# Mixer heads: VectorE weighs each tile of scores within the turn that made its argument

## The chip, the cores and the metric

The kernel runs on one core of a Trainium2 chip. TensorE (PE in the profile; its weight loads are PEld) multiplies matrices, VectorE (DVE), ScalarE (ACT) and GpSimd (POOL) work on tiles, and SyncE (SP) issues the DMAs. The engines run side by side, each through its own list of instructions in order, and wait for each other at semaphores. The metric is the device time of one execution in microseconds (us); lower is better.

## What is computed

The reference runs two blocks of a model over 512 tokens of width 1024. The change lies in the first block's token mixer, in the four heads of its gated linear attention. In the reference's chunked form this is, for each head and each chunk:

```python
d = jnp.where(causal, b[..., :, None] - b[..., None, :] + logi[..., None, :], -jnp.inf)
m_t = jnp.maximum(inter, jnp.max(d, -1))
p = jnp.exp(d - m_t[..., None]) * jnp.einsum('bhctd,bhcsd->bhcts', q, k)
num = (s_int[..., None] * jnp.einsum('bhcvk,bhctk->bhctv', c_prev, q)
       + jnp.einsum('bhcts,bhcsv->bhctv', p, v))
den = s_int * jnp.einsum('bhck,bhctk->bhct', n_prev, q) + jnp.sum(p, -1)
h = num / jnp.maximum(jnp.abs(den), jnp.exp(-m_t))[..., None]
```

The heads are then standardized over their 128 features (mean and variance), scaled, and multiplied by a sigmoid gate. The kernel has no chunks here: it takes all 512 tokens of a head at once, so that `p` is one causal matrix, and `num` and `den` are its products with the values and with ones.

## The kernel before

**Tiles and turns.** Everything is feature-major, 128 partitions by up to 512 columns. The causal matrix of a head is worked in four tiles of 128 keys by 512, 384, 256 and 128 queries. One tile is a turn; `n` counts the 16 turns, `h, j = divmod(n, 4)` is the head and the tile in it. All engines run through the same loop over `n` in `mlstm`, each with its own part:

- VectorE makes the tile's argument (`argument`, L1535 and L1536) in `e[:, n % 4]` (tile `m_e`), which frees ScalarE to take its exponential (L1684).
- TensorE makes the scores in one of two PSUM banks (L1579).
- VectorE weighs: `weigh(n)` multiplies scores and exponential (L1522, scores from PSUM) and then the first 128 columns with the causal mask (L1524, two inputs in SBUF), and reports `prob_ready`.
- TensorE multiplies the tile with the values (L1417) and with ones (L1418), in `nums(n)`, one turn later. In turn n it runs: the scores of n, four steps of a fill, `nums(n - 1)`, a sum for the norm of the head before, a product for the pair, four more steps of a fill.

**What else stands in a turn.** The *fill* is a projection of the block's input (3 products a step, L435 to L437) with streamed weights, one job of eight steps a turn; VectorE takes most of them out of PSUM (`shifted`, L1809 and L1811), ScalarE every fourth. The *norm* of head h - 1 runs through the turns of head h in steps 0 to 3 (`norm_values`: L1498 in step 1, L1503 and L1505 in step 2, the reciprocal L1509 in step 3), and `norm_end` (L1512, L1514) ends it in the turn after. The *pair* is the preparation of the next stage's operands (`Operands.dve`), one pair per four turns: in turns with j = 1 its step 0 (L1888 to L1898, which waits for gates from ScalarE, after TensorE's L1836 and L1852), with j = 2 step 1 (L1902, behind a root of ScalarE's, and the reciprocal L1903), with j = 3 step 2 (L1905, L1906, L1908), and with j = 0 of the next head step 3 (L1913, L1914, L1915, L1920). L1908 is what TensorE's L1845 waits for, which stands in a turn with j = 0 between the scores and the fill.

**Streamed weights.** In each turn ScalarE, after its exponential, casts the high part of the next weights' tile (L387), and GpSimd makes its low part behind that (L396, both inputs in SBUF, 128x1024). SyncE loads the tile after next as a slot of the ring becomes free.

**What sets the order.** The order is written by hand: on each engine the instructions run as the loops give them out, and every dependency is a semaphore. In VectorE's loop before, turn n begins with `weigh(n - 1)`, then come `argument(n)`, `norm_end`, the take of the fill's job, `norm_values` and the pair's step. In the last turn, n = 15, `weigh(15)` stands behind the take as well.

Of the kernel before, what the change touches and what calls it, by code (L numbers as in the profile page):

```python
# [30 lines left out]
ST = S // P  # L31
# [6 lines left out]
MW, MH, MHD = 512, 4, 128  # L38
# [1308 lines left out]
def mlstm(k, h_in, arriving, early, qk, v, o, rkv, wa, gd, lora, lora_g, pairs, rooms, core, raw, norm):  # L1347
# [57 lines left out]
    def prep(n):  # L1405

        return [(pairs[(n - 1) // ST], (n - 1) % ST)] if 0 < n <= MH * ST else []
# [86 lines left out]
    def norm_values(dve, chain, h, step):  # L1494
        if step == 1:

            dve.wait_ge(*meaned.ge(2 * h + 1))
            nc.vector.scalar_tensor_tensor(out=hm[:], in0=k.banks[SPREAD], scalar=-1.0 / MHD, in1=hm[:],  # L1498
                                           op0=ALU.mult, op1=ALU.add).then_inc(*G("centred_ready").inc())
        if step == 2:  # L1500

            dve.wait_ge(*G("den_ready").ge(h + 1))
            chain(nc.vector.tensor_tensor(rs, rs, lowb[:], ALU.max))  # L1503
            dve.wait_ge(*meaned.ge(2 * h + 2))
            nc.vector.scalar_tensor_tensor(out=rs, in0=k.banks[SPREAD], scalar=1.0 / MHD, in1=rs,  # L1505
                                           op0=ALU.mult, op1=ALU.add).then_inc(*G("var_ready").inc())
        if step == 3:
            dve.wait_ge(*rooted.ge(h + 1))
            chain(nc.vector.reciprocal(rs, rs))  # L1509

    def norm_end(dve, chain, h):
        chain(nc.vector.scalar_tensor_tensor(out=hm[:], in0=hm[:], scalar=k.vec("m_norm_g", h), in1=rs, op0=ALU.mult, op1=ALU.mult))  # L1512
        dve.wait_ge(*fill.taken(names.index(f"o{h}")))
        nc.vector.tensor_tensor(y[:, h, :], hm[:], o[:, h, :], ALU.mult).then_inc(*normed.inc())  # L1514

    def weigh(dve, chain, n):
        h, j = divmod(n, ST)
        ed = e[:, n % 4, 0:width[j]]

        dve.wait_ge(*expd.ge(n + 1))  # L1520
        dve.wait_ge(*sent.ge(n + 1))
        chain(nc.vector.scalar_tensor_tensor(out=ed, in0=k.banks[SCORE[n % 2]][:, 0:width[j]], scalar=MHD ** -0.5, in1=ed,  # L1522
                                             op0=ALU.mult, op1=ALU.mult))
        nc.vector.tensor_tensor(e[:, n % 4, 0:P], e[:, n % 4, 0:P], k.const("key_le_query"), ALU.mult).then_inc(*prob.inc())  # L1524

    def argument(dve, chain, n):
        h, j = divmod(n, ST)
        if j == 0:

            dve.wait_ge(*G("spread_taken").ge(top_nth(h)))  # L1530
        if n >= 4:

            dve.wait_ge(*summed.ge(n - 3))
        ed = e[:, n % 4, 0:width[j]]
        chain(nc.vector.tensor_scalar(ed, topb[:, j * P:S], u_col[:, j, h:h + 1], -1.0, ALU.subtract, ALU.mult))  # L1535
        nc.vector.tensor_scalar(ed, ed, 0.0, None, ALU.min).then_inc(*made.inc())  # L1536

    with k.stage() as block:
        @block.sync
        def _(sp):  # L1540
            k.load_inputs(sp)
            k.prefetch(sp, fill.first[GATES_JOB])
            k.load_tables(sp)
            k.load_small(sp, lora[:], k.lora[:, 0, :])
            k.load_small(sp, lora_g[:], k.lora[:, 1:3, :])
            k.lora_landed = k.small_load()
            k.prefetch(sp, k.used)

            sp.wait_ge(*G("operands_made").ge(PAIRS))
            sp.wait_ge(*G("values_made").ge(2 * PAIRS))  # L1550
            k.load_small(sp, raw, k.memT)
            k.raw_landed = k.small_load()
# [166 lines left out]
        @block.vector  # L1719
        def _(dve):  # L1720
            chain = Chain(dve, G("dve_step"))
            nc.vector.memset(hm[:, 0:1], 0.0).then_inc(*G("gains_ready").inc())
            early.dve(dve, 0, 4)
            k.split_first(dve)
            early.dve(dve, 4, DT)
            arriving.dve_adds(dve, 0, 4)
            arriving.dve_adds(dve, 4)
            arriving.dve_roots(dve)

            dve.wait_ge(*arriving.named("turned_ready").ge(1))  # L1730
            nc.vector.tensor_copy(hm[:], k.banks[arriving.turn_bank]).then_inc(*G("high_made").inc())
            arriving.dve_parts(dve, 0, DT)
            c = VECTORS["mu_rkv"]
            chain(nc.vector.tensor_scalar(k.keep_share[:], k.vecs[:, c:c + 15], -1.0, 1.0, ALU.mult, ALU.add))
            for t in range(2 * MH):
                fill.take(dve, chain, t)
            fill.take(dve, chain, GATES_JOB)
            dve.wait_ge(*G("gate_taken").ge(1))
            nc.vector.scalar_tensor_tensor(out=tmp, in0=fpre, scalar=-1.0, in1=fpre, op0=ALU.mult,
                                           op1=ALU.max).then_inc(*G("abs_ready").inc())  # L1740
            fill.take(dve, chain, WA)

            dve.wait_ge(*G("ln_ready").ge(1))
            chain(nc.vector.scalar_tensor_tensor(out=fpre, in0=fpre, scalar=0.0, in1=tmp, op0=ALU.min, op1=ALU.subtract))
            chain(nc.vector.tensor_tensor_scan(run, fpre, fpre, 0.0, ALU.add, ALU.bypass))
            nc.vector.tensor_tensor(u, ipre, run, ALU.subtract).then_inc(*G("rows_ready").inc())
            dve.wait_ge(*G("rows_ready").ge(1))
            chain(nc.vector.tensor_tensor_scan(top, u, u, 0.0, ALU.max, ALU.max))
            nc.vector.tensor_tensor(low, top, run, ALU.add).then_inc(*G("rows_ready").inc())

            dve.wait_ge(*G("floor_ready").ge(1))
            chain(nc.vector.tensor_scalar(low, low, EPS, 1e-37, ALU.mult, ALU.max))
            nc.vector.tensor_scalar(low, low, 1e37, None, ALU.min).then_inc(*G("floor_ready").inc())

            dve.wait_ge(*G("turned_ready").ge(1))
            nc.vector.tensor_copy(u_col[:].rearrange("p t h -> p (t h)"), k.banks[SPREAD][:, 0:ST * MH]).then_inc(*G("turned_taken").inc())
            dve.wait_ge(*G("turned_taken").ge(1))
            dve.wait_ge(*k.tables_landed)
            for n in range(MH * ST):
                h, j = divmod(n, ST)  # L1760
                if n:
                    weigh(dve, chain, n - 1)
                argument(dve, chain, n)
                if h >= 2 and j == 0:
                    norm_end(dve, chain, h - 2)
                if n and jobs[UNITS + n - 1].engine == "dve":
                    fill.take(dve, chain, UNITS + n - 1)
                if n == MH * ST - 1:
                    weigh(dve, chain, n)
                if h:  # L1770
                    norm_values(dve, chain, h - 1, j)
                if n == MH * ST - 1:
                    norm_end(dve, chain, h - 1)
                for pair, step in prep(n):
                    pair.dve(dve, step, arrived)
            fill.take(dve, chain, LAST)
            norm_values(dve, chain, MH - 1, 1)
            last_pair.dve(dve, 3, arrived)
            core.dve_masks(dve, 0, 0, 0)
            norm_values(dve, chain, MH - 1, 2)  # L1780
            core.dve_masks(dve, 0, 0, 1)
            core.dve_masks(dve, 0, 0, 2)
            norm_values(dve, chain, MH - 1, 3)
            norm_end(dve, chain, MH - 1)
            for step in range(3):
                core.dve_masks(dve, 0, 1, step)
            core.dve_rest(dve, 0)
            core.dve_group(dve, 1)
# [2622 lines left out]
```

## Time and profile before

| | |
|---|---|
| median of 3 runs | 1659.35 us (1658.65 to 1659.6) |
| the profiled execution's own time | 1663.44 us |
| its span in the trace | 1661.6 us |
| TensorE busy | 1597.8 us, 96% |
| VectorE busy | 911.7 us, 55% |
| ScalarE busy | 690.3 us, 42% |
| GpSimd busy | 712.0 us, 43% |
| mean granted clock of TensorE | 0.994 |

The heads run from about 97 to 256 us of the span. A busy share over the whole span says little of them: what matters there is which wait ends last in each turn. The trace's timeline gives each instruction its start, its length, its line, and in brackets how long its engine sat idle before it and which instruction let it go. Matmul ends are modelled and overlap; the distance between two starts on TensorE is the surer measure. A row of waits adds up such idle times for one pair of lines. The profiled execution took 4.1 us more than the median; a difference worked out from its rows is set against its own time and then carried to the median.

### The profile page before, as it was taken

To read this page: it belongs to the slowest core of one execution; us is meant where nothing else is said; L and a number is where in the kernel's file an instruction comes from. 1 tells how busy PE (TensorE), PEld (TensorE's weight loads), DVE (VectorE), ACT (ScalarE), POOL (GpSimd) and SP (SyncE) were. 2 spreads that over 40 slices of the span, in tenths; PEclk is the share of its full clock that TensorE was granted. 3 is DMA by queue.
4 is the path that set the end of the run, shared out by engine and by line. 5 is a ranking of instruction groups with operands and counts; after the bars stand their busy time and mean duration, and the time that the engine had idled before them with its cause. 6 is when DMAs were issued, how large, how long until landed. Compare 5 with 4: busy or idle time off the path is not lost. (4 is left out here: it accounts for less than half of the span.)

```text
span 1661.6 us, 25020 instructions
## 1 busy us (share of the span) xinstructions
PE 1597.8 (96%) x10298; PEld 1229.7 (74%) x10298; DVE 911.7 (55%) x1464; ACT 690.3 (42%) x1184; POOL 712.0 (43%) x357
## 2 busy tenths in 40 slices
PE   6999998879999899999999999999999999999999
PEld 5876666778887688888888888476676567787787
DVE  5957878446852427556531157697536663324251
ACT  5544454324432532222233234434645465455441
POOL 4533336234652145555564446343134422463342
PEclk9999999999999999999999999999999999999999
DMA  5321111003432032333333343022112210442132
GB/s 183 137 87 51 51 51 54 4 29 91 153 113 76 26 102 76 95 96 101 102 92 105 95 133 118 23 64 64 41 57 75 89 64 26 139 156 86 51 100 79
DMA packets 39713, 138.54 MB, mean 83 GB/s; under 512 B 4400, under 2 KB 5680, under 8 KB 38320
## 3 DMA queue, kind: packets, MB, share of 16 engines
q1 hardware_dynamic: 39600, 136.94, 26.1%
q8 instruction: 82, 1.34, 0.3%
q14 instruction: 31, 0.25, 0.1%
HBM read 132.73 MB, written 4.19 MB: 82 GB/s over the span
## 5 line engine op out<-in xcount | busy, mean ns | idle before, releaser
L396 POOL TENSOR_TENSOR parts<-ring,parts 128x1024 fp32r<-128x1024 f32 (+3 forms) x250 | 581.8, 2333 | 806.6 <-ACT parts L387 806.5
L435 PE MATMUL banks<-h_hi,parts 128*128 128x512 f32 x1120 | 461.9, 412 | 3.4 <-PEq L295 3.4
L437 PE MATMUL banks<-h_hi,parts 128*128 128x512 f32 x1120 | 438.1, 391 | 0.0
L436 PE MATMUL banks<-h_lo,parts 128*128 128x512 f32 x1120 | 437.6, 391 | 0.0
L387 ACT CAST parts<-ring 128x1024 fp32r<-128x1024 f32 (+3 forms) x251 | 244.8, 979 | 134.9 <-PE banks L437 134.8
L435 PEld LDWEIGHTS banks<-h_hi,parts 128*128 128x128 f32 x1120 | 211.4, 189 | 62.4 <-issue 18.7
L436 PEld LDWEIGHTS banks<-h_lo,parts 128*128 128x128 f32 x1120 | 211.5, 189 | 46.1 <-issue 5.1
L437 PEld LDWEIGHTS banks<-h_hi,parts 128*128 128x128 f32 x1120 | 210.9, 188 | 45.2
L3130 ACT CAST ffn_act_hi<-ffn_gate 128x512 fp32r<-128x512 f32 x22 | 13.7, 622 | 162.7 <-DVE ffn_gate L3029 162.7
L435 PE MATMUL banks<-ffn_act_hi,parts 128*128 128x512 f32 x176 | 68.5, 389 | 0.0
L436 PE MATMUL banks<-ffn_act_lo,parts 128*128 128x512 f32 x176 | 68.5, 389 | 0.0
L437 PE MATMUL banks<-ffn_act_hi,parts 128*128 128x512 f32 x176 | 68.5, 389 | 0.0
L3086 DVE TENSOR_TENSOR ffn_raw<-banks,ffn_root 128x512 f32<-128x512 f32 x22 | 15.2, 691 | 86.9 <-PE banks L437 86.8
L3096 DVE TENSOR_TENSOR x<-x,banks 128x512 f32<-128x512 f32 x8 | 5.5, 687 | 88.5 <-PE banks L437 88.5
L1074 DVE SCALAR_TENSOR_TENSOR ffn_gate<-ffn_raw,vecs,ffn_gate 128x511 f32<-128x511 f32 (+1 forms) x44 | 52.5, 1192 | 1.6
L2753 ACT ACTIVATE scores<-scores,row_stats 128x128 f32<-128x128 f32 (+3 forms) x64 | 35.5, 555 | 29.9 <-DVE row_stats L2731 29.8
L1070 DVE TENSOR_SCALAR ffn_gate<-ffn_raw,vecs 128x512 f32<-128x512 f32 x22 | 40.4, 1836 | 0.8
L435 PEld LDWEIGHTS banks<-ffn_act_hi,parts 128*128 128x128 f32 x176 | 33.0, 188 | 6.9
L436 PEld LDWEIGHTS banks<-ffn_act_lo,parts 128*128 128x128 f32 x176 | 33.0, 188 | 6.9
L437 PEld LDWEIGHTS banks<-ffn_act_hi,parts 128*128 128x128 f32 x176 | 33.0, 188 | 6.7
L2741 DVE TENSOR_SCALAR scores<-scores,row_stats 128x128 f32<-128x128 f32 (+3 forms) x64 | 34.6, 540 | 2.3
L2793 ACT ACTIVATE h_hi<-x,vecs 128x512 fp32r<-128x512 f32 x16 | 11.6, 726 | 51.3 <-DVE x L3075 27.1
(607 smaller groups left out, 2979.4 us busy)
## 6 DMA issues: line engine op xcount, KB each, us to landing
ring<-weights SPq DMA_DIRECT2D x211, 512.0 KB, 3.5
ring<-weights SPq DMA_DIRECT2D x24, 256.0 KB, 2.6
x<-xT SPq DMA_DIRECT2D x4, 1024.0 KB, 5.4
ring<-weights SPq DMA_DIRECT2D x8, 384.0 KB, 3.1
x_spill<-x SPq DMA_DIRECT2D x2, 1024.0 KB, 4.8
x<-x_spill SPq DMA_DIRECT2D x1, 2048.0 KB, 9.2
outT<-x SPq DMA_DIRECT2D x8, 256.0 KB, 2.0
ring<-weights SPq DMA_DIRECT2D x8, 192.0 KB, 2.4
```

The costliest lines, as they stand in the source:

```text
L387: self.nc.scalar.copy(self.parts[:, t % PARTS, 0, 0:w], self.ring[:, t % SLOTS, 0:w]).then_inc(self.high_ready, 1)
L396: self.nc.gpsimd.tensor_tensor(self.parts[:, t % PARTS, 1, 0:w], self.ring[:, t % SLOTS, 0:w], self.parts[:, t % PARTS, 0, 0:w].bitcast(F3 ...
L435: nc.tensor.matmul(out, w.hi, x.hi, start=first, stop=False)
L436: nc.tensor.matmul(out, w.hi, x.lo, start=False, stop=False)
L437: return nc.tensor.matmul(out, w.lo, x.hi, start=False, stop=last)
L1070: chain(nc.vector.tensor_scalar(dst, bank, k.vec(f"{weights}{taps - 1}", tile), k.vec(bias, tile), ALU.mult, ALU.add))
L1074: ins = nc.vector.scalar_tensor_tensor(out=dst[:, lag:S], in0=bank[:, 0:S - lag], scalar=k.vec(f"{weights}{j}", tile), in1=dst[:, lag:S], ...
L2741: nc.vector.tensor_scalar(scores(j - 1, e), scores(j - 1, e), st[:, 3:4], None, ALU.mult).then_inc(*scaled.inc())
L2753: nc.scalar.activation(scores(j, e), scores(j, e), ACT.Exp, bias=small[:, u % NS, 1:2], scale=-1.0, accum_out=small[:, u % NS, 2:3]).then_ ...
L2793: nc.scalar.mul(self.h.hi[:, m, :], k.x[:, m, :], k.vec(self.gain, m)).then_inc(*G("h_high").inc())
L3086: nc.vector.tensor_tensor(r, bank(gate_job(f)), root, ALU.mult).then_inc(*G("gate_taken").inc())
L3130: nc.scalar.copy(act_t.hi[:, f, :], gate[:, f % GATES, :]).then_inc(*G("act_high").inc())
```

## The change

VectorE's loop loses `weigh(n - 1)` at the turn's start. `weigh(n)` now stands, in every turn, behind the take of the fill's job and ahead of `norm_values` and of the pair's step; for the last turn this is where it was. The weighing of turn n thus waits for the exponential and the scores of the same turn. No instruction is added or removed, and the other engines' lists are the same.

```diff
             for n in range(MH * ST):
                 h, j = divmod(n, ST)
-                if n:
-                    weigh(dve, chain, n - 1)
                 argument(dve, chain, n)
                 if h >= 2 and j == 0:
                     norm_end(dve, chain, h - 2)
                 if n and jobs[UNITS + n - 1].engine == "dve":
                     fill.take(dve, chain, UNITS + n - 1)
-                if n == MH * ST - 1:
-                    weigh(dve, chain, n)
+                weigh(dve, chain, n)
                 if h:
                     norm_values(dve, chain, h - 1, j)
                 if n == MH * ST - 1:
```

Lines behind the edit stand three lower in the changed kernel (L1809 becomes L1806, L1902 becomes L1899, L1908 becomes L1905). VectorE's instructions in turn 6 (head 1, j = 2), before; the first two rows weigh turn 5:

```order
L1522 SCALAR_TENSOR_TENSOR m_e<-banks,m_e 128x384
L1524 TENSOR_TENSOR m_e<-m_e,consts 128x128
L1535 TENSOR_SCALAR m_e<-top_b,u_col 128x256
L1536 TENSOR_SCALAR m_e<-m_e 128x256
L1809 TENSOR_SCALAR rkv<-banks,keep_share 128x512
L1811 SCALAR_TENSOR_TENSOR rkv<-banks,vecs,rkv 128x511
L1503 TENSOR_TENSOR y<-y,floor_b 128x512
L1505 SCALAR_TENSOR_TENSOR y<-banks,y 128x512
L1902 TENSOR_SCALAR x<-x 128x512
L1903 RECIPROCAL x<-x 128x512
```

And now, from the argument of turn 6 on; the weighing is that of turn 6:

```order
L1535 TENSOR_SCALAR m_e<-top_b,u_col 128x256
L1536 TENSOR_SCALAR m_e<-m_e 128x256
L1806 TENSOR_SCALAR rkv<-banks,keep_share 128x512
L1808 SCALAR_TENSOR_TENSOR rkv<-banks,vecs,rkv 128x511
L1522 SCALAR_TENSOR_TENSOR m_e<-banks,m_e 128x256
L1524 TENSOR_TENSOR m_e<-m_e,consts 128x128
L1503 TENSOR_TENSOR y<-y,floor_b 128x512
L1505 SCALAR_TENSOR_TENSOR y<-banks,y 128x512
L1899 TENSOR_SCALAR x<-x 128x512
L1900 RECIPROCAL x<-x 128x512
```

The weighing of 384 columns left the turn's start, and that of 256 columns stands between the fill's take (L1808) and the norm's L1503. VectorE in turn 7 (j = 3), before:

```order
L1522 SCALAR_TENSOR_TENSOR m_e<-banks,m_e 128x256
L1524 TENSOR_TENSOR m_e<-m_e,consts 128x128
L1535 TENSOR_SCALAR m_e<-top_b,u_col 128x128
L1536 TENSOR_SCALAR m_e<-m_e 128x128
L1809 TENSOR_SCALAR rkv<-banks,keep_share 128x512
L1811 SCALAR_TENSOR_TENSOR rkv<-banks,vecs,rkv 128x511
L1509 RECIPROCAL y<-y 128x512
L1905 TENSOR_TENSOR x<-x 128x512
L1906 TENSOR_TENSOR qk_60<-qk_60,x 128x512
L1908 SCALAR_TENSOR_TENSOR x<-rkv,vecs,x 128x512
```

And now:

```order
L1535 TENSOR_SCALAR m_e<-top_b,u_col 128x128
L1536 TENSOR_SCALAR m_e<-m_e 128x128
L1806 TENSOR_SCALAR rkv<-banks,keep_share 128x512
L1808 SCALAR_TENSOR_TENSOR rkv<-banks,vecs,rkv 128x511
L1522 SCALAR_TENSOR_TENSOR m_e<-banks,m_e 128x128
L1524 TENSOR_TENSOR m_e<-m_e,consts 128x128
L1509 RECIPROCAL y<-y 128x512
L1902 TENSOR_TENSOR x<-x 128x512
L1903 TENSOR_TENSOR qk_60<-qk_60,x 128x512
L1905 SCALAR_TENSOR_TENSOR x<-rkv,vecs,x 128x512
```

The weighing of turn 7 (128 columns) now stands directly ahead of the norm's reciprocal L1509, and that of turn 6 has left the turn.

## Rows read from the trace of the kernel before

**Rows 1.** Waits, 97 to 256 us: who waited for whom, us in total, times, longest.
```profile
DVE m_hm L1498 <- PE banks L1473: 13.4, 3, 6.0
...
PEld banks L1417 <- DVE m_e L1524: 6.7, 8, 1.2
...
PE banks L1417 <- DVE m_e L1524: 3.3, 8, 0.8
```

**Rows 2.** TensorE's timeline: start us, us, engine, line, operation, tiles, shape, [idle before <-releaser].
```profile
132.75 1.97 PE L1845 MATMUL banks<-x,consts 128*128 128x512 f32 x2
...
156.24 0.91 PE L1417 MATMUL banks<-m_e,m_v 128*128 128x384 f32 x2 [0.36 <-DVE m_e L1524]
...
165.60 0.70 PE L1417 MATMUL banks<-m_e,m_v 128*128 128x256 f32 x2 [0.34 <-DVE m_e L1524]
...
173.00 1.12 PE L1845 MATMUL banks<-x,consts 128*128 128x512 f32 x2 [0.37 <-DVE x L1908]
...
211.60 2.07 PE L1845 MATMUL banks<-x,consts 128*128 128x512 f32 x2 [0.36 <-DVE x L1908]
...
565.56 0.47 PE L435 MATMUL banks<-x_out_parts_hi,parts 128*128 128x512 f32 x1 [2.81 <-DVE x_out_parts_lo L1145]
```

**Rows 3.** VectorE's timeline, turns 2 and 3, 6 and 7, and 15.
```profile
120.70 0.84 DVE L1902 TENSOR_SCALAR x<-x 128x512 f32<-128x512 f32 x1 [1.89 <-ACT x L1869]
...
128.25 2.80 DVE L1906 TENSOR_TENSOR x<-x 128x512 f32<-128x512 f32 x1
...
155.31 0.56 DVE L1522 SCALAR_TENSOR_TENSOR m_e<-banks,m_e 128x384 f32<-128x384 f32 x1
...
155.90 0.29 DVE L1524 TENSOR_TENSOR m_e<-m_e,consts 128x128 f32<-128x128 f32 x1
...
156.11 0.35 DVE L1535 TENSOR_SCALAR m_e<-top_b,u_col 128x256 f32<-128x256 f32 x1
...
157.48 0.75 DVE L1811 SCALAR_TENSOR_TENSOR rkv<-banks,vecs,rkv 128x511 f32<-128x511 f32 x1
...
158.14 0.68 DVE L1503 TENSOR_TENSOR y<-y,floor_b 128x512 f32<-128x512 f32 x1
...
160.74 0.64 DVE L1902 TENSOR_SCALAR x<-x 128x512 f32<-128x512 f32 x1 [1.18 <-ACT x L1869]
...
164.79 0.42 DVE L1522 SCALAR_TENSOR_TENSOR m_e<-banks,m_e 128x256 f32<-128x256 f32 x1
...
165.46 0.28 DVE L1535 TENSOR_SCALAR m_e<-top_b,u_col 128x128 f32<-128x128 f32 x1
...
167.37 3.34 DVE L1509 RECIPROCAL y<-y 128x512 f32<-128x512 f32 x1
...
172.19 0.75 DVE L1908 SCALAR_TENSOR_TENSOR x<-rkv,vecs,x 128x512 f32<-128x512 f32 x1
...
172.86 0.28 DVE L1522 SCALAR_TENSOR_TENSOR m_e<-banks,m_e 128x128 f32<-128x128 f32 x1
...
246.48 2.26 DVE L1524 TENSOR_TENSOR m_e<-m_e,consts 128x128 f32<-128x128 f32 x1
```

**Rows 4.** ScalarE's timeline, turn 6.
```profile
157.14 1.03 ACT L387 CAST parts<-ring 128x1024 fp32r<-128x1024 f32 x1
```

**Rows 5.** GpSimd's timeline, turns 6 and 7.
```profile
158.24 2.85 POOL L396 TENSOR_TENSOR parts<-ring,parts 128x1024 fp32r<-128x1024 f32 x1 [12.81 <-ACT parts L387]
...
167.36 2.42 POOL L396 TENSOR_TENSOR parts<-ring,parts 128x1024 fp32r<-128x1024 f32 x1 [6.27 <-ACT parts L387]
```

**Rows 6.** GpSimd's timeline, turn 15.
```profile
246.16 2.44 POOL L396 TENSOR_TENSOR parts<-ring,parts 128x1024 fp32r<-128x1024 f32 x1 [6.27 <-ACT parts L387]
```

**Rows 7.** Busy time by stretch: stretch, length, each engine (instructions), PEclk, DMA share, GB/s.
```profile
130.00:140.00 10.00, 10.00 (x31) 5.81 (x30) 9.79 (x14) 3.73 (x6) 5.52 (x4) 0.83 0.28 84
210.00:220.00 10.00, 9.64 (x33) 6.49 (x33) 9.76 (x15) 3.24 (x5) 4.76 (x3) 0.83 0.29 93
565.00:575.00 10.00, 9.44 (x34) 7.64 (x35) 5.90 (x10) 5.62 (x11) 2.56 (x1) 0.83 0.16 54
```

## The prediction

> **What bounds the kernel now.** I read the waits of the mixer's heads first [rows 1], then TensorE's timeline there [rows 2], then VectorE's, ScalarE's and GpSimd's [rows 3 to 6], and the granted clock last [rows 7]. In the waits, TensorE's product of the weighed scores (L1417) waited 8 times of 16 for the mask product L1524, which ends the weighing: 6.7 us in its weight loads and 3.3 us in its matmuls [rows 1]. That is what the change can give back. VectorE had 13.4 us of waiting of its own at L1498, in three pieces, so it is not full over the whole region [rows 1].
>
> TensorE's timeline shows where each wait lies. Call a head's four turns j = 0 to 3. In head 1 the waits are at 156.24 us (turn 6, j=2, 0.36 us) and at 165.60 us (turn 7, j=3, 0.34 us), and then a third, 0.37 us at 173.00 (turn 8), which is for another VectorE row: L1908, the last of the pair's step [rows 2]. So in turns 6 and 7 TensorE and VectorE are nearly level. VectorE's rows there follow each other almost without a pause: from 155.31, where L1522 begins, to 172.94, where L1908 ends (172.19 + 0.75), it idles only 1.18 us, at L1902, for a root that ScalarE makes from what VectorE gave it [rows 3]. L1845 on TensorE starts 0.06 us behind L1908's end. **The chain that sets a head's length in its second half is VectorE's, up to L1908.** Its first half, from L1845 to the next gates, is TensorE's fills. L1845 to L1845 took 38.60 us (173.00 to 211.60) and 40.25 us (132.75 to 173.00) [rows 2].
>
> **The change part by part.** Nothing is added or removed: 16 weighings, two VectorE instructions each, move from the start of turn n+1 to turn n, behind the argument and the taking out of a fill. Seen from a turn's start, the argument comes earlier and the weighing later.
>
> *The eight waits at L1417.* The weighing that they wait for is now done a turn earlier; even with all that follows, it is over some 5 us ahead. They go. At 0.36 and 0.34 us of idle matmul time, and up to 6.7/8 = 0.84 us of weight-load time each [rows 1, 2], I take 0.55 us: 1.1 us a head. In heads 1 to 3 this is only worth something if L1908 is not late, since L1845 waits for it already.
>
> *Turn 6 on VectorE (and turns 10, 14).* Before, L1535 began at 156.11, 0.80 us behind the turn's start at 155.31; now it begins at the start, so everything that hangs on it comes 0.80 us earlier: the exponential, the cast L387 of the next weights (157.14, now 156.34), and behind it GpSimd's L396 (158.24, now 157.44) [rows 3 to 5]. The fill's L1811 ended at 158.23, now at 157.43. L1522 can start 0.09 us ahead of that end, as L1503 does now (158.14), so at 157.34; at 0.42 us for 256 columns it ends at 157.76, and L1524 starts at 157.80. L396 has been running for 0.36 us by then. What that does the trace shows: the L1524 at 246.48 took 2.26 us instead of 0.29, and ended 0.14 us behind the L396 that had begun at 246.16 (end 248.60) [rows 3, 6]. So did L1906 at 128.25, 2.80 us against the 0.68 of L1503, which has the same shape [rows 3]. Hence L1524 ends at 157.44 + 2.42 + 0.14 = 160.00, with 2.42 us the undisturbed L396 of 167.36 [rows 5]. L1503 then starts at 159.91, where it was at 158.14 (it got in 0.1 us ahead of L396): **1.77 us later**, and the root, L1902 and the reciprocal with it.
>
> That rule is also in the Trainium skill (SBUF — State Buffer, section Who interferes with whom): a VectorE instruction with two SBUF inputs and a GpSimd one that reads SBUF exclude each other for a whole instruction, and whichever starts first decides. It speaks against this change; the trace agrees by the 2.26 us above. If the two did not exclude each other, the stalls would be zero and the sum -1.6 us (worked out under the rivals).
>
> *Turn 7 (and 11).* Here the argument was 0.67 us behind the turn's start (165.46 against 164.79). L396 goes from 167.36 to 166.69. The reciprocal L1509 stood at 167.37, right behind the fill's take; without the 0.67 us it could start at 166.70. There L1522 now stands, 0.28 us for 128 columns (172.86) [rows 3], and L1524 at 167.02, 0.33 us behind L396's start. It ends at 166.69 + 2.42 + 0.14 = 169.25, and L1509 starts at 169.17: **1.80 us later**. L1522 has one SBUF input (the other is in PSUM), L1509 one; neither is held up.
>
> *Turns 8, 12 (j=0) and 5, 9, 13 (j=1).* The weighing is now ahead of L1913 to L1920 and may be stalled by the rest of an L396 too, but VectorE has its waits at L1498 right behind it, 13.4 us in three [rows 1]. Cost zero; if that cover were gone, up to 2.4 us a head. In j=1 no fill is taken by VectorE, and L1524 comes before L396: zero.
>
> *Head 0 (turns 1 to 4).* In turn 2 VectorE waited 1.89 us for the root at L1902 [rows 3], which covers the stall of 1.77 us. In turn 3, L1906 at 128.25 already lost its 2.1 us to the same L396; now L1524 loses them in its place. Nothing is lost, and the two waits at L1417 are given back: -1.1 us.
>
> *Head 3.* Turn 14 pays 1.77 us. Turn 15 already weighed twice, the second time stalled (the 2.26 us); it loses one weighing, 0.7 us. The waits of two products go, 1.1 us. I take 0 for the sum.
>
> Queues: SP issues weights behind the low parts that L396 makes, which move by under 1 us per turn; no DMA is in these waits, so zero.
>
> Sum: -1.1 + 2 x (1.77 + 1.80) + 0 = -1.1 + 7.1 = **+6.0 us** on the profiled execution's 1663.4 us. Applied to the median of 1659.35 us this is 1665.4 us. What follows the heads is bound by TensorE and VectorE in sequence, so I carry the shift through. Bounds of the one unknown size, the stall: from nothing (L1524 ahead of L396) to 2.42 us; per head 0 to 4.8 us.
>
> **The clock.** In two stretches, 130 to 140 and 210 to 220 us, the mean granted clock was 0.83 [rows 7]: a spell at the lower of the two levels (1.2 GHz). The head with the first took 1.65 us more (40.25 against 38.60 us). After the change TensorE pauses at L1845 in heads 1 and 2 for 0.37 + 0.70 + 3.57 = 4.6 us at a time. A pause of 2.81 us at 565.56 was followed by a stretch of 0.83 [rows 2, 7]. Two new spells, at 1.65 us, would add 3.3 us; two spells are there already, and the first may go, as the work shifts. I leave the number at two in the forecast and keep 3.3 us for the range.
>
> The Trainium skill (TensorE: Matmul & The Clock Gate, section Part 1: The HAM clock gate) says that an idle TensorE falls to half its clock and wins it back by work. By that the long pauses would each bring a spell, and the sum would be 9.3 us in place of 6.0.
>
> **The rivals.**
>
> *VectorE comes first.* If L396 starts over 0.36 us later than I shift it (turn 6; 0.33 us in turn 7), L1524 is through before it. For it: L1503 won just such a race by 0.1 us, at 158.14. Against it: cast and L396 both hang on the argument, as L1524 does, so the 0.36 us is a difference of fixed durations. Then a head's chain is shorter by 0.09 + 0.13 us; TensorE's waits still move to L1845, since VectorE's chain sets the pace: -1.1 - 0.5 = -1.6 us, 1657.8 us. Chance 0.08. If it wins in one of the two turns only: 6.0 - 3.6 = +2.4 us, 1661.8 us, chance 0.12.
>
> *All waits are kept as gain.* If the chain to L1908 has a slack that I don't see, the eight waits give between 3.3 and 6.7 us; 5 us, 1654.4 us. Against it: L1845 waits for L1908 already. It decides if L1908 ends no later than now by more than 0.37 us. Chance 0.06.
>
> *The stalls come, and the pauses slow the clock.* +6.0 + 3.3 = 1668.7 us. Chance 0.24, as part of slower.
>
> *The order does nothing,* because ScalarE's exponential comes too late for VectorE: no, the cast behind the exponential of turn 6 starts at 156.34, 1.1 us before the fill is taken out (157.43).
>
> **How the numbers follow.** Forecast (stalls, two spells) 0.50 at 1665.4; its own range 1664 to 1667. Stalls with slower clock 0.24. One of the stalls 0.12, none 0.08, all waits kept 0.06. A measurement of this kernel can tell some 0.2% (3.3 us) from no change, so faster 0.06, same 0.20, slower 0.74. The range runs from 1659.0 to 1669.5: it leaves out the cases at 1657.8 and 1654.4 and a little at the top.
>
> **What would show it.** In the changed kernel's trace L1524 in turns 2, 3, 6, 7, 10, 11, 14 lasts about 2.2 us and ends 0.14 us behind an L396. L1417 waits for nothing; TensorE's idle time ahead of L1845 is over 3 us in heads 1 and 2. L1845 to L1845 takes some 42.2 us from head 1 to 2, where it took 38.60. I am wrong if L1524 lasts 0.29 us in those turns, if L1845's waits stay under 1 us, or if something behind the heads gives the 6 us back.

## The result

The changed kernel is slower, by more than forecast.

| | before | changed |
|---|---|---|
| median | 1659.35 us (5 runs, 1658.65 to 1662.48) | 1672.32 us (5 runs, 1669.93 to 1673.57) |
| ratio | | 1.0065, 95% interval 1.0047 to 1.0083 |
| profiled execution: time, span | 1663.44, 1661.6 us | 1669.98, 1668.2 us |
| mean granted clock, profiled | 0.994 | 0.990 |

A second comparison on one chip with other kernels gave 1670.65 us against 1660.68 us, ratio 1.0054 (1.0039 to 1.0069). By the two ratios the loss is 10.8 and 9.0 us, by the plain medians 13.0 and 10.0 us, where I had said 6.0; the time lies above the range. The two profiled executions are only 6.5 us apart: that of the kernel before was slower than all five of its timed runs, that of the changed kernel is its second fastest. So the traces below show where the time goes, but not all of the loss.

**VectorE, turns 6 and 7 of the changed kernel** (start us, length us, engine, line), which answer to [rows 3]; lines behind the edit stand three lower (L1902 is now L1899, L1908 is L1905). Turn 6 begins with L1535, at 153.69:

```profile
153.69 0.35 DVE L1535 TENSOR_SCALAR m_e<-top_b,u_col 128x256 f32<-128x256 f32 x1
...
155.07 0.75 DVE L1808 SCALAR_TENSOR_TENSOR rkv<-banks,vecs,rkv 128x511 f32<-128x511 f32 x1
...
155.74 0.41 DVE L1522 SCALAR_TENSOR_TENSOR m_e<-banks,m_e 128x256 f32<-128x256 f32 x1
...
156.18 2.21 DVE L1524 TENSOR_TENSOR m_e<-m_e,consts 128x128 f32<-128x128 f32 x1
...
158.32 0.68 DVE L1503 TENSOR_TENSOR y<-y,floor_b 128x512 f32<-128x512 f32 x1
...
160.91 0.43 DVE L1899 TENSOR_SCALAR x<-x 128x512 f32<-128x512 f32 x1 [1.18 <-ACT x L1866]
...
164.76 0.28 DVE L1535 TENSOR_SCALAR m_e<-top_b,u_col 128x128 f32<-128x128 f32 x1
...
166.67 0.28 DVE L1522 SCALAR_TENSOR_TENSOR m_e<-banks,m_e 128x128 f32<-128x128 f32 x1
...
166.98 2.23 DVE L1524 TENSOR_TENSOR m_e<-m_e,consts 128x128 f32<-128x128 f32 x1
...
169.14 3.34 DVE L1509 RECIPROCAL y<-y 128x512 f32<-128x512 f32 x1
...
173.96 0.75 DVE L1905 SCALAR_TENSOR_TENSOR x<-rkv,vecs,x 128x512 f32<-128x512 f32 x1
```

**GpSimd there**, which answers to [rows 5]:

```profile
155.84 2.41 POOL L396 TENSOR_TENSOR parts<-ring,parts 128x1024 fp32r<-128x1024 f32 x1 [9.92 <-ACT parts L387]
...
166.67 2.40 POOL L396 TENSOR_TENSOR parts<-ring,parts 128x1024 fp32r<-128x1024 f32 x1 [8.42 <-ACT parts L387]
```

L1524 takes 2.21 and 2.23 us where it took 0.29 us, and both times L396 began ahead of it, by 0.34 and 0.31 us. Nothing else in these turns has grown: L1522 waits for nobody, and the wait for the root at L1899 is 1.18 us, as it was. Over the 16 turns L1524 takes 2.17 to 2.25 us in turns 2, 3, 4, 6, 7, 10, 11, 14 and 15, 1.72 us in turn 1, 0.72 to 0.77 us in turns 0, 8 and 12, and 0.29 us in turns 5, 9 and 13.

**TensorE.** The waits of the changed kernel, 97 to 266 us (us in total, times, longest), against [rows 1]:

```profile
PEld banks L1842 <- DVE x L1905: 12.4, 3, 5.8
...
DVE m_hm L1498 <- PE banks L1473: 10.8, 3, 4.4
...
PE banks L1842 <- DVE x L1905: 10.0, 2, 5.0
...
DVE m_e L1522 <- ACT m_e L1684: 1.8, 3, 0.6
```

L1417 is gone from the list. VectorE's wait for the exponential in the argument's own turn (L1522 for L1684) is 1.8 us in all, in three places, in turns 5, 9 and 13. L1417's place in the list is taken by L1842 (L1845 before). Its four places in TensorE's timeline, against [rows 2]:

```profile
132.79 1.13 PE L1842 MATMUL banks<-x,consts 128*128 128x512 f32 x2
...
174.77 2.07 PE L1842 MATMUL banks<-x,consts 128*128 128x512 f32 x2 [5.01 <-DVE x L1905]
...
218.29 2.08 PE L1842 MATMUL banks<-x,consts 128*128 128x512 f32 x2 [4.98 <-DVE x L1905]
...
264.53 1.02 PE L1842 MATMUL banks<-x,consts 128*128 128x512 f32 x2
```

From L1842 to L1842 it now is 41.98 us (132.79 to 174.77) and 43.52 us (174.77 to 218.29), where it was 40.25 and 38.60 us. Around the second and third product the mean granted clock stood at 1.00 and 0.83 before (170 to 180, 210 to 220 us). In the changed kernel it is (stretch, length, busy time of each engine, PEclk, DMA share, GB/s):

```profile
130.00:140.00 10.00, 10.00 (x37) 6.22 (x36) 9.83 (x13) 3.83 (x6) 4.49 (x4) 1.00 0.30 79
170.00:180.00 10.00, 5.23 (x14) 3.55 (x15) 9.76 (x13) 1.95 (x3) 2.75 (x2) 0.66 0.16 52
215.00:225.00 10.00, 6.71 (x21) 4.80 (x22) 9.76 (x14) 1.94 (x3) 3.70 (x2) 0.66 0.12 33
```

The level is the lower one (1.2 GHz) from 171.2 to 178.1 us and from 215.6 to 222.4 us: each spell begins in the pause ahead of L1842, and ends 3.3 and 4.1 us behind the product's start. Before, the two spells lasted 3.4 us each (from 132.9 and from 211.4 us).

### The profile page after: what moved, and what is told of

Its sections match the earlier page's. It is cut to its first block and busy times, and to the rows that moved or that the text cites. A ratio compares the mean times of both kernels' runs of the same rounds, so it can differ in the third digit from the quotient of the medians.

```text
span 1668.2 us, 25026 instructions
## 1 busy us (share of the span) xinstructions
PE 1599.5 (96%) x10298; PEld 1233.2 (74%) x10298; DVE 919.7 (55%) x1464; ACT 690.9 (41%) x1184; POOL 706.7 (42%) x357
## 5 line engine op out<-in xcount | busy, mean ns | idle before, releaser
L396 POOL TENSOR_TENSOR parts<-ring,parts 128x1024 fp32r<-128x1024 f32 (+3 forms) x250 | 575.8, 2309 | 819.5 <-ACT parts L387 819.3
L1074 DVE SCALAR_TENSOR_TENSOR ffn_gate<-ffn_raw,vecs,ffn_gate 128x511 f32<-128x511 f32 (+1 forms) x44 | 48.3, 1097 | 1.6
L1070 DVE TENSOR_SCALAR ffn_gate<-ffn_raw,vecs 128x512 f32<-128x512 f32 x22 | 44.2, 2011 | 0.8
```

The source lines that it names most:

```text
L396: self.nc.gpsimd.tensor_tensor(self.parts[:, t % PARTS, 1, 0:w], self.ring[:, t % SLOTS, 0:w], self.parts[:, t % PARTS, 0, 0:w].bitcast(F3 ...
L1070: chain(nc.vector.tensor_scalar(dst, bank, k.vec(f"{weights}{taps - 1}", tile), k.vec(bias, tile), ALU.mult, ALU.add))
L1074: ins = nc.vector.scalar_tensor_tensor(out=dst[:, lag:S], in0=bank[:, 0:S - lag], scalar=k.vec(f"{weights}{j}", tile), in1=dst[:, lag:S], ...
```

## Experiments

My theory: (1) L1524 is held behind L396 in the turns with j = 2 and 3, (2) that makes L1905 late and TensorE stands at L1842, and (3) its pauses lower the granted clock, which comes on top. The rivals: that weighing in the argument's own turn costs time by itself (VectorE waits for the exponential, or the pair's work comes late), and that the part of the loss that I had not forecast lies behind the heads. "Before" in each comparison is the kernel before on the same chip.

### e1: the two rows out of L396's way

```diff
-        chain(nc.vector.scalar_tensor_tensor(out=ed, in0=k.banks[SCORE[n % 2]][:, 0:width[j]], ...))
-        nc.vector.tensor_tensor(e[:, n % 4, 0:P], e[:, n % 4, 0:P], k.const("key_le_query"), ALU.mult)
+        score = k.banks[SCORE[n % 2]]
+        chain(nc.vector.tensor_tensor(score[:, 0:P], score[:, 0:P], k.const("key_le_query"), ALU.mult))
+        nc.vector.scalar_tensor_tensor(out=ed, in0=score[:, 0:width[j]], scalar=MHD ** -0.5, in1=ed, ...)
...
                 argument(dve, chain, n)
+                if h and j == 2:
+                    norm_floor(dve, chain, h - 1)
```

`norm_floor` is L1503, taken out of `norm_values` for all heads but the last.

> The changed kernel with VectorE's two rows that met GpSimd's L396 taken out of its way: the causal mask is multiplied into the scores in PSUM ahead of the weighing (so that neither row of the weighing has two SBUF inputs), and the norm's L1503 stands right behind the argument, ahead of L396. If the stalls behind L396 are the cause, the 1.8 us in the turns with j = 2 and in those with j = 3 go, 7 us in heads 1 and 2, and the pauses of 5.0 us ahead of L1842 shrink to about 1.5 us, with the low clock behind them: 1657 to 1660 us, the weighing's second row without any length over 0.8 us. If instead the wait for ScalarE's exponential in the same turn, or something behind the heads, costs the time, it stays at 1670 to 1673 us.

Measured: 1659.79 us against 1660.80 us, ratio 0.9991 (0.9981 to 1.0002). VectorE in turn 7 of e1, where the weighing is now L1527 (mask into the scores in PSUM) and L1528, with the reciprocal L1513 behind it, and GpSimd's L396 beside them:

```profile
164.66 0.29 DVE L1527 TENSOR_TENSOR banks<-banks,consts 128x128 f32<-128x128 f32 x1
...
164.99 0.29 DVE L1528 SCALAR_TENSOR_TENSOR m_e<-banks,m_e 128x128 f32<-128x128 f32 x1
...
165.20 3.34 DVE L1513 RECIPROCAL y<-y 128x512 f32<-128x512 f32 x1
...
164.66 2.42 POOL L396 TENSOR_TENSOR parts<-ring,parts 128x1024 fp32r<-128x1024 f32 x1 [6.50 <-ACT parts L387]
```

The weighing stands at the same place as in the changed kernel, L396 runs beside it, and neither row is held: 0.29 us each. TensorE's pauses ahead of the pair's product (L1849 here) are 1.17 and 1.16 us. The order that the change makes costs nothing by itself; the rows with two SBUF inputs that met L396 did. This takes the first rival away.

What I had not expected is that the low clock did not go with the long pauses. In this execution a spell of 3.4 us begins at 171.8 us, behind the pause of 1.17 us, and one of 6.8 us at 209.3 us, at the pause of 1.16 us; 5.6 us of it lie behind the product:

```profile
170.83 1.18 PE L1849 MATMUL banks<-x,consts 128*128 128x512 f32 x2 [1.17 <-DVE x L1912]
...
210.00:220.00 10.00, 9.46 (x30) 7.04 (x31) 9.37 (x15) 3.04 (x5) 5.33 (x3) 0.69 0.17 52
```

### e2: TensorE kept busy in the pauses

The changed kernel with idle products inside the pauses; they compute nothing that is used.

```diff
                 for pair, step in prep(n):
                     if step == 3:
+                        if n in (8, 12):
+                            pe.wait_ge(*G("rooted").ge(pair.p + 1))
+                            for _ in range(18):
+                                nc.tensor.matmul(k.banks[7], h_in.hi[:, 0, 0:P], h_in.hi[:, 0, :], start=True, stop=True)
                         pair.pe(pe, 2)
```

> The changed kernel with 18 idle products (128x512, into the bank that L1842 overwrites) on TensorE ahead of L1842 in turns 8 and 12, some 4.1 us each, inside the pauses of 5.0 us. The stalls on VectorE stay. If the low granted clock behind the two pauses is what made the loss larger than the 6 us of the stalls, the spells of 6.8 us at half clock are gone and the time is 1664 to 1668 us. If the rest of the loss lies behind the heads or in the stalls themselves, it stays at 1670 to 1673 us.

Measured: 1667.19 us against 1660.80 us, ratio 1.0038 (1.0025 to 1.0051). TensorE's timeline at the first pause (L1588 is the idle product, L1846 the pair's), and the granted clock in the same stretches as above:

```profile
169.35 4.38 PE L1588 MATMUL banks<-h_hi 128*128 128x512 f32 x18
...
174.41 1.13 PE L1846 MATMUL banks<-x,consts 128*128 128x512 f32 x2 [0.68 <-DVE x L1909]
...
216.37 1.13 PE L1846 MATMUL banks<-x,consts 128*128 128x512 f32 x2 [0.67 <-DVE x L1909]
```

```profile
130.00:140.00 10.00, 10.00 (x38) 6.41 (x37) 9.79 (x14) 3.83 (x6) 4.49 (x4) 1.00 0.31 97
170.00:180.00 10.00, 9.32 (x42) 7.08 (x41) 9.76 (x13) 2.70 (x5) 3.10 (x2) 1.00 0.15 51
215.00:225.00 10.00, 9.33 (x41) 6.94 (x40) 9.79 (x15) 2.66 (x4) 5.43 (x3) 1.00 0.17 54
```

The stalls on VectorE are all there, but no spell of low clock is left in the heads. From L1846 to L1846 it is 41.96 us (174.41 to 216.37) where the changed kernel had 43.52: 1.56 us of clock. From the third to the fourth it is 44.32 us (216.37 to 260.69) against 46.24 us (218.29 to 264.53): 1.92 us. So 3.5 us of the changed kernel's time in these two pieces are the clock's, and with idle work in their place the loss is 6.4 us; its interval, 4.2 to 8.5 us, holds the 6.0 that the stalls were forecast to cost. The intervals of the ratios of e2 and of the changed kernel overlap slightly. The trace separates them, and so does the clock of the timed runs: 0.994 to 0.997 in the six of e2, 0.989 to 0.993 in the eleven of the changed kernel.

### e3: the weighings of j = 0 and 1 moved alone

The edit is shown against the changed kernel.

```diff
+            moved = lambda n: n % ST < 2 or n == MH * ST - 1
...
+                if n and not moved(n - 1):
+                    weigh(dve, chain, n - 1)
                 argument(dve, chain, n)
...
-                weigh(dve, chain, n)
+                if moved(n):
+                    weigh(dve, chain, n)
```

> One part of the change alone: the weighing moves into its own turn only for j = 0 and 1 (and turn 15, where it was); for j = 2 and 3 it stays at the next turn's begin. By the theory of the stalls none is left, since the moved weighings of j = 1 come before L396 and those of j = 0 lie in VectorE's slack, and L1908's chain loses the weighing of 0.8 us at the begin of the turn with j = 2: -2 to -3 us against the kernel before, 1656 to 1658 us. If moving any weighing ahead of the pair's work costs time (the operands late), it is slower than before, 1662 us or more.

Measured: 1656.36 us against 1660.80 us, ratio 0.9974 (0.9964 to 0.9985): clearly faster than before. In its trace L1524 takes 0.29 us in turns 5 to 7, and TensorE waits 0.35 us for the pair's product; from product to product it is 37.82 us (172.92 to 210.74), 0.78 us less than before:

```profile
172.92 1.13 PE L1846 MATMUL banks<-x,consts 128*128 128x512 f32 x2 [0.35 <-DVE x L1909]
```

That is the weighing of 384 columns (0.80 us from L1522 to L1535), which left the begin of the turn with j = 2. I had expected no stall at all, and that is not so: L1524 still takes 2.19 and 2.22 us in turns 1 and 4 and 0.79 us in turns 8 and 12. Each of these is followed by a longer wait of VectorE's own (1.6 us in head 0, 4.3 us at L1498 in head 1, 1.9 us there in head 2), so they do not reach the product.

### e4: TensorE asks later

The changed kernel with the pair's product behind the fill's four steps and `nums`.

```diff
-                for pair, step in prep(n):
-                    if step == 3:
-                        pair.pe(pe, 2)
                 fill.pe(pe, 4)
                 if n:
                     nums(pe, n - 1)
+                for pair, step in prep(n):
+                    if step == 3:
+                        pair.pe(pe, 2)
```

> The changed kernel with TensorE's L1842, which waits for VectorE's L1905, moved behind four steps of the fill and the products of the weighed scores (about 3.2 us of other work). The stalls on VectorE stay. If what makes the kernel slower is that TensorE stands at L1842, each of heads 1 and 2 wins about 3.2 us back and the pauses shrink to under 2 us, with fewer spells of low clock: 1660 to 1664 us. If VectorE's stalls cost the time through another wait, it stays at 1670 to 1673 us.

Measured: 1658.88 us against 1660.80 us, ratio 0.9991 (0.9979 to 1.0004), better than the 1660 to 1664 us that I expected. The pauses are 1.59 and 1.62 us, and no spell of low clock lies in the heads:

```profile
172.99 1.12 PE L1842 MATMUL banks<-x,consts 128*128 128x512 f32 x2 [1.59 <-DVE x L1905]
...
170.00:180.00 10.00, 8.41 (x37) 6.34 (x36) 9.76 (x15) 2.55 (x4) 3.82 (x3) 1.00 0.12 27
```

VectorE's stalls are the same as in the changed kernel. What made them so dear is that TensorE stood at L1842 with the rest of its work behind it. They are not free here either: from product to product it is 38.81 us (172.99 to 211.80), against 36.93 us in e10 below, where they are gone. I did not run this edit on the kernel before; e8 against e3 below shows it to be worth nothing that could be measured where there are no long pauses.

### e5 and e6: the whole change again, and the weighing of j = 3 alone

e5 is the changed kernel itself.

> The changed kernel itself once more, beside the others of this call, since the first comparison had 5 runs. Ratio 1.005 to 1.008 against before, 1666 to 1673 us, with at least one spell of 6.8 us of low clock that begins in a pause ahead of L1842.

Measured: 1670.65 us against 1660.68 us, ratio 1.0054 (1.0039 to 1.0069). The pauses are 4.97 and 4.94 us, and a spell of 6.8 us begins in each, at 171.7 and 216.0 us.

e6 is e3 with `moved = lambda n: n % ST == 3`.

> The other part of the change alone: only the weighing of j = 3 moves into its own turn, ahead of the reciprocal L1509. By the theory of the stalls its second row starts about 0.3 us behind L396 and is held for some 2 us, which puts L1509 2.4 us later in heads 1 and 2 (turns 7 and 11), pauses of 3 us ahead of L1845 follow, and the clock adds 1 to 3 us: 1664 to 1669 us. If only the turns with j = 2 matter, where two rows of VectorE stand behind the stall for a root of ScalarE, it is 1658 to 1661 us.

Measured: 1672.97 us against 1660.68 us, ratio 1.0062 (1.0046 to 1.0078). That is above what I expected, and as slow as the whole change. The stall is as worked out: in turn 7 L1524 starts 0.31 us behind L396 and is held, and L1509 starts 5.07 us behind the turn's begin (164.65), where it was 2.58 us.

```profile
164.65 0.42 DVE L1522 SCALAR_TENSOR_TENSOR m_e<-banks,m_e 128x256 f32<-128x256 f32 x1
...
167.53 2.27 DVE L1524 TENSOR_TENSOR m_e<-m_e,consts 128x128 f32<-128x128 f32 x1
...
169.72 3.34 DVE L1509 RECIPROCAL y<-y 128x512 f32<-128x512 f32 x1
...
167.22 2.44 POOL L396 TENSOR_TENSOR parts<-ring,parts 128x1024 fp32r<-128x1024 f32 x1 [6.28 <-ACT parts L387]
```

```profile
170.00:180.00 10.00, 7.12 (x14) 3.62 (x14) 9.79 (x11) 2.74 (x4) 2.16 (x1) 0.68 0.18 53
215.00:225.00 10.00, 7.16 (x15) 4.39 (x16) 9.79 (x12) 2.15 (x3) 3.65 (x2) 0.66 0.14 39
```

Two things make it as slow as the whole change. Head 0 gives nothing back: from the first L1579 to the first product it is 33.58 us (99.03 to 132.61), as before, where the whole change takes 31.91 us; so 2.5 us a head here come to the same as 3.4 us a head less 1.7 us there. And the clock again: the pause is only 2.88 us, but of the spell that begins at 173.6 us 5.1 us lie behind its end at 175.36. The period is 43.50 us (175.36 to 218.86). VectorE's two turns account for 2.5 us over the 38.60 us of before, so some 2.4 us are the clock's, more than the 1.6 us behind the pause of 5 us.

### e7: the edits of e1 on the kernel before

> The kernel before with the two edits of e1 (mask multiplied into the scores in PSUM, L1503 right behind the argument), as a control: they should be worth little where the weighing stands at the turn's begin, since only the stalls in turns 1, 5 and 15 go: 1658 to 1661 us. If they give 2 us or more by themselves, then e1 says less of the stalls than it seems.

Measured: 1658.86 us against 1660.68 us, ratio 0.9990 (0.9981 to 1.0000). So e1's 10 us against the changed kernel are not a gain of the edits as such: where the weighing stands at the turn's begin, they give 0.1%, and 0.2% at the interval's end.

### e9: the weighing ahead of the fill's take

```diff
                 argument(dve, chain, n)
...
+                weigh(dve, chain, n)
                 if n and jobs[UNITS + n - 1].engine == "dve":
                     fill.take(dve, chain, UNITS + n - 1)
-                weigh(dve, chain, n)
```

> The changed kernel with one thing other: in each turn the weighing stands ahead of the fill's take, not behind it. VectorE then waits some 0.4 us for the exponential, but L1524 is through before L396 starts. By the theory of the stalls L1509 in turns 7 and 11 is only 0.4 us later than before the change, where it was 1.8 us; L1503 in turns 6 and 10 now meets L396 itself and ends 1.6 us later than before the change. Sum 2 x 2.0 - 1.1 = 2.9 us, and 0 to 3 us of clock: 1662 to 1666 us, with L1524 at 0.29 us in the turns with j = 2 and 3. If weighing in the argument's own turn is what costs, wherever it stands, it is 1669 us or more.

Measured: 1667.13 us against 1659.97 us, ratio 1.0044 (1.0027 to 1.0060), a little above what I expected. VectorE in turns 6 and 7, TensorE's product behind them, and GpSimd's L396 of turn 6:

```profile
153.07 0.42 DVE L1522 SCALAR_TENSOR_TENSOR m_e<-banks,m_e 128x256 f32<-128x256 f32 x1 [0.48 <-ACT m_e L1684]
...
153.53 0.29 DVE L1524 TENSOR_TENSOR m_e<-m_e,consts 128x128 f32<-128x128 f32 x1
...
155.18 1.82 DVE L1503 TENSOR_TENSOR y<-y,floor_b 128x512 f32<-128x512 f32 x1
...
163.69 0.29 DVE L1522 SCALAR_TENSOR_TENSOR m_e<-banks,m_e 128x128 f32<-128x128 f32 x1 [0.38 <-ACT m_e L1684]
...
164.01 0.30 DVE L1524 TENSOR_TENSOR m_e<-m_e,consts 128x128 f32<-128x128 f32 x1
...
165.67 3.34 DVE L1509 RECIPROCAL y<-y 128x512 f32<-128x512 f32 x1
...
171.31 2.08 PE L1842 MATMUL banks<-x,consts 128*128 128x512 f32 x2 [3.34 <-DVE x L1905]
...
154.05 2.41 POOL L396 TENSOR_TENSOR parts<-ring,parts 128x1024 fp32r<-128x1024 f32 x1 [10.27 <-ACT parts L387]
```

L1524 is at 0.29 and 0.30 us in the same turn as its argument, after waits for the exponential of 0.48 and 0.38 us; L1503, which starts 1.13 us behind L396, pays instead: 1.82 us where it took 0.68. An instruction that the diff never touches is held or free by where it falls against L396. From L1842 to L1842 it is 43.05 us (171.31 to 214.36); VectorE's turns 6 and 7 are 1.7 us longer than before (10.85 and 7.74 us to L1905, against 9.48 and 7.40 us), so the clock has 2.7 us of it, behind a pause of 3.34 us.

### e8, e10, e11: versions that beat both kernels

e8 is e3 with e4's edit, e10 the whole change with those of e1 and e4, e11 is e8 with those of e1.

> e3 (weighing moved for j = 0 and 1 alone) together with e4 (L1845 behind four steps of the fill). The chain to L1908 stays as in e3, but TensorE does 3 us of other work before it asks for it, so the second half of a head no longer stands still for VectorE: 1652 to 1656 us. If TensorE is full by now in the heads, it is as e3, 1656 to 1658 us.

> The whole change, with the stalls taken out (e1) and L1842 behind other work of TensorE's (e4). Neither VectorE's chain nor TensorE's wait for it should be left: 1652 to 1656 us, pauses under 1 us in the heads. If it is no faster than e1 and e4 (1659 to 1660 us), the heads are bound by something that neither touches.

> e8 (weighing moved for j = 0 and 1 alone, L1845 later) with the edits of e1. The edits of e1 alone were worth 0.1% on the kernel before; here the same 1 to 2 us at most: 1653 to 1656 us, the fastest of all by little or level with e8.

| kernel | median us | before us | ratio | 95% interval |
|---|---|---|---|---|
| e3 | 1656.36 | 1660.80 | 0.9974 | 0.9964 to 0.9985 |
| e8 | 1655.36 | 1660.68 | 0.9973 | 0.9958 to 0.9988 |
| e10 | 1653.77 | 1659.97 | 0.9969 | 0.9957 to 0.9981 |
| e11 | 1653.85 | 1659.97 | 0.9963 | 0.9949 to 0.9978 |

e8, e10 and e11 came out where expected, and their intervals do not separate them from each other or from e3. e10 is the changed kernel's own order: with L1524's second SBUF input gone, L1503 ahead of L396 and TensorE asking later, it is 0.3% faster than the kernel before, where the change alone was 0.5 to 0.65% slower. From product to product it takes 36.93 us (172.62 to 209.55), and TensorE waits nowhere over 0.5 us in the heads.

## Why the prediction was wrong

**The direction and the mechanism held.** Point by point:

- *The eight waits at L1417 go.* They did; none is left in the waits.
- *Turn 6: L396 0.36 us ahead of L1524.* Measured 0.34 us. L1503 was to be 1.77 us later from the turn's begin; it is 1.80 us later (158.32 - 153.69 = 4.63 us, against 158.14 - 155.31 = 2.83 us).
- *Turn 7: 0.33 us ahead, L1509 1.80 us later.* Measured 0.31 us, and 1.80 us (169.14 - 164.76 = 4.38 us, against 167.37 - 164.79 = 2.58 us).
- *3.57 us a head.* 3.36 us in e2, where the clock stays out of it (41.96 - 38.60), and 3.38 us in head 1 of the changed kernel, whose low level up to the second product lies in the pause (41.98 - 38.60). The 0.2 us between them are L1899, which took 0.64 us before and takes 0.43 us now (160.91); it had itself begun beside L396. The 42.2 us that I forecast from L1845 to L1845 in head 2 are 41.96 us in e2, and 43.52 us with the clock.
- *Head 0 gives 1.1 us.* From the first L1579 to the first L1845 it was 33.60 us (99.15 to 132.75) and is 31.91 us (100.88 to 132.79): 1.7 us less.
- *Head 3 nets to zero.* From the third product to the transposes behind the heads (L2005, now L2002) it was 55.80 us (211.60 to 267.40) and is 55.60 us (218.29 to 273.89), with a spell of low clock in each, 3.2 us of it before and 4.1 us now.
- *The shift is carried through.* At these transposes the profiled execution is 6.5 us later than before; at its end, 6.6 us. Nothing behind the heads gave it back or added to it, which takes the second rival away for this pair of executions. The 6.5 us are 1.7 ahead of the heads, where the changed kernel's execution has a spell (from 96.1 us) and that of before has none, -1.7 in head 0, +1.7 in head 1, whose 40.25 us before had a spell in them, +4.9 in head 2, and -0.2 behind.

**The step that failed is the term for the clock, which the forecast had at nothing.** I wrote: "I leave the number at two in the forecast and keep 3.3 us for the range." The number of spells in the heads did stay at two, but each was 6.8 us where it had been 3.4 us, and in both profiled executions of the changed kernel they came in the two pauses. Against e2, which has none, they cost 1.56 and 1.92 us, 3.5 us together. In the profiled pair this hardly shows, since the two spells of before had cost about as much (1.65 us in head 1, and half of the 3.2 us behind the third product). Over the timed runs it does: the mean granted clock fell from 0.994 or 0.995 to 0.990 (0.989 to 0.992 in the five runs). Of 1660 us, 0.004 to 0.005 of the clock is 7 to 8 us at full clock. Of the changed kernel's two spells 3.6 and 2.7 us fall into the pauses, where they cost nothing; that is 3.1 us of it, and 4 to 5 us are left, by this estimate. The loss by the ratios less e2's 6.4 us is 2.6 to 4.4 us. Where the spells of the timed runs lie, no trace shows.

The 3.3 us that I kept for the range were near the right size, but I gave them a chance of 0.24, and even that case, 1668.7 us, lies 3.6 us below the median. Two further terms are on record. The base was low: the five runs of before had 1659.35 us, over 28 and 23 later runs the median was 1660.8 and 1660.7 us, which is 1.4 us. The stalls less the gains were put 1.1 us too high: -1.7 in head 0, 3.4 in each of heads 1 and 2 and -0.2 in head 3 come to 4.9 us, not 6.0. With 4 to 5 us of clock the sum is 1670 to 1671 us. The repeat, 1670.65 us, is there; the first comparison is 1 to 2 us above, and the interval of its ratio is 3 us to either side.

My own rows spoke for the dearer case: the pause of 2.81 us at 565.56 was followed by a stretch of 0.83, and I forecast pauses of 4.6 us (measured 5.0). The rule of the Trainium skill that I named (TensorE: Matmul & The Clock Gate, section Part 1: The HAM clock gate) says that an idle TensorE falls to half its clock. The traces agree: each of the eight pauses of 2.8 to 5.0 us ahead of this product (two each in the changed kernel, its repeat, e6 and e9) has a spell. By it the sum was 9.3 us, and 9.0 and 10.8 us were measured; that this comes so near is in part luck, as the 6.0 us in it for the stalls were 1 us too many.

What a pause costs beyond its length follows from where its spell lies. For the second product and the period from it to the third, "low behind it" is the time at the low level in this period while TensorE is not in a pause:

| kernel | pause us | period us | low behind it us | of it clock us |
|---|---|---|---|---|
| before | 0.37 | 38.60 | 0 | 0 |
| e2 | 0.68 | 41.96 | 0 | 0 |
| e1 | 1.17 | 39.71 | 3.4 | 1.6 |
| e4 | 1.59 | 38.81 | 0 | 0 |
| e6 | 2.88 | 43.50 | 5.1 | 2.4 |
| e9 | 3.34 | 43.05 | 5.9 | 2.7 |
| changed | 5.01 | 43.52 | 3.3 | 1.6 |

The last column is worked out from the periods alone: the changed kernel less e2's 41.96 us, e1 less its own period before, which has no spell (38.14 us), e6 and e9 less 38.60 us and what VectorE's two turns grew by (2.5 and 1.7 us). It is half of the column before it, or a little less. The longer pause is not the dearer one: in a pause of 5 us more of the low level is spent while TensorE waits anyway. And a short pause does not rule a spell out: e1's pauses of 1.2 us have one, e4's of 1.6 us have none. Why, no run here shows.

What stays open is the clock outside the heads. In e6's profiled execution there are three spells between 334 and 389 us where the kernel before has one, and I can't say why; part of e6's 12 us may be there.

## What to carry to other kernels

When an instruction of VectorE with two SBUF inputs is moved, look at what GpSimd runs at the new place, and shift GpSimd's own start with the edit: an event that hangs on the moved rows moves too. Here a difference of 0.3 us decided over 1.8 us, twice in each head. Taking one of the two inputs from PSUM, by changing the order of two multiplications, removes the question. And where the trace of before has spells of low clock behind pauses, put them into the sum for a new pause and not only into the range: here a pause of 2.9 to 5.0 us cost 1.6 to 2.7 us on top of its length. Or give TensorE other work ahead of the product that waits.

## What was not expected of the hardware

- A pause of 2.9 or 3.3 us cost more clock (2.4 and 2.7 us) than one of 5.0 us (1.6 us); the low spells were 6.8 us long in all three, and also at a pause of 1.2 us in e1.
- A product from PSUM and SBUF ran at 0.29 us with L396 beside it, where one from two SBUF tiles of the same size took 2.2 us (e1 and the changed kernel). The held one ended 0.14 us behind L396 in each of turns 6 and 7.
- A VectorE row with one SBUF input (512 columns, a maximum with a constant) took 0.64 us where it began 0.35 us ahead of L396's end (L1902 before) and 0.43 us without L396 (L1899 now).
